# The end of a transformer kernel: last expert's output by halves, look-ahead behind the branch, one residual instruction and one store per tile

## The chip, the cores and the metric

The kernel runs on one core of a Trainium2 chip. The metric is the time of one execution on the device in microseconds (us); lower is better. The engines that matter here are TensorE (PE, matmuls), VectorE (DVE) and ScalarE (ACT) for elementwise work, GpSimd (POOL), and SyncE (SP), which issues transfers. Each runs its own queue of instructions in order; they wait for each other through semaphores.

## The reference

Two layers of a block that mixes differential attention and gated linear attention, for 256 latent tokens beside 256 context tokens, width 1024, fp32. The second layer's feed-forward part is a mixture of 8 experts, two per token. Only its end matters here:

```python
logits = (ht @ router).astype(jnp.float32)
top_v, top_i = lax.top_k(logits, TOP_K)                  # TOP_K = 2 of 8 experts
wts = jax.nn.softmax(top_v, axis=-1)
combine = jnp.sum(one_hot(top_i, 8) * wts[..., None], axis=1)
def expert_step(acc, p):
    e1, e3, e2, cw = p                                   # 1024x2816, 1024x2816, 2816x1024
    return acc + cw[:, None] * swiglu(ht, e1, e3, e2), None
out, _ = lax.scan(expert_step, jnp.zeros_like(ht), (w1, w3, w2, combine.T))
x = x + gt2 * rms_norm(out, g_post_ffn[l])               # out: 256 x 1024, the result is x
```

`rms_norm(y, g)` is y * rsqrt(mean(y*y) + 1e-6) * g, the mean over the 1024 columns of a token. In the kernel gt2 * g is one row, `gate`, copied to all partitions.

## The kernel before, in words

Tokens lie on the 128 partitions, so 256 tokens are two tiles (t = 2 and 3 of `X`, tt = 0 and 1 of `y_moe`). Matmuls run in fp32r with each operand split in a high and a low part: `three` (L1444) does hi*hi, hi*lo, lo*hi, three matmuls of 128x512. ACT makes high parts (`high`, L917: w_hi <- raw), DVE low parts (`low`, L1327: raw minus w_hi).

**Experts.** Weights come in units of 128x2048 (1 MB), 33 per expert, through 5 places for raw data and 4 for split ones. An expert is one pass p over at most 128 of its tokens; three extra passes (8, 9, 10) exist for experts with more. A pass has 11 column chunks g: `up_chunk` (two units into a PSUM bank), ACT's silu, DVE's product, PE's transposes (`turn_chunk`), `down_chunk` (one unit: 12 matmuls that add to the two PSUM banks of the pass, one for each half of 512 output columns). PE starts by gathering the pass's tokens and later scatters the output back.

**Look-ahead.** ACT and DVE split the unit that is 4 ahead of the one just used: `high(ahead(...))` and `low(ahead(...))` in `run`. Behind the last down chunk of a run they so split a unit of the next pass, though nothing may need it.

**Output of a pass** (`output`, L937 and L1341): ACT copies each half out of PSUM as ey_hi, DVE makes ey_lo. PE multiplies both by the transposed selection (`scatter`, L1796), four pieces n = 2*tt + h, and DVE adds each, times the token's weight, to `y_moe` (`added`, L1349). For passes 0 to 7 this happens inside the next pass.

**Runs and the branch.** Passes 0 to 7 are one run; each extra pass is a run of its own inside nested `If(run_valid(eng, k))` (L492): the engine loads a register from `task_i` (`TENSOR_LOAD`), tests it and branches. Every engine has its own such branch. In the `Else` stands the end: the last output, four scatters into four banks, four accumulations.

**The tail.** `mean_square` (L675 Square with sums to `ssq`, L678 Sqrt) on ACT; `residual` (L1227) on DVE: reciprocal, y * rstd * gate, and for tile 3 the addition to X; POOL adds tile 2 (L578); SP stores both tiles in one transfer (L567).

The order of the instructions on each engine is the order of the code; no scheduler changes it.

## Time and profile before

| | us |
|---|---|
| three timed runs | 2032.96, 2034.84, 2035.08 |
| their median | 2034.84 |
| the profiled execution, its own time | 2033.05 |
| its span in the trace | 2030.9 |

| engine | busy us | share of the span |
|---|---|---|
| PE | 1885.3 | 93% |
| DVE | 1242.8 | 61% |
| ACT | 1068.4 | 53% |
| POOL | 43.6 | 2% |

The rows further down come from one profiled execution. All times in them are us from the start of its span unless marked ns. The engines overlap, so shares of busy time don't add up to the span; a serial stretch shows as idle times that end with another engine's instruction.

### The profile page before, as it was taken

How to read it: one execution, taken by the hardware profiler on the slowest of the kernel's cores; microseconds unless marked ns; L12 is line 12 of the kernel's file. 1: busy time of each engine (PE TensorE's matmuls, PEld its weight loads, DVE VectorE, ACT ScalarE, POOL GpSimd, SP SyncE). 2: the span in 40 equal slices, each digit the busy share in tenths (PEclk: the TensorE clock that was granted, in tenths of full speed). 3: DMA queues.
4: the chain of work that ended last, by engine and by line, in shares of the span. 5: the costliest groups of instructions: out<-in, count | busy, mean ns of one | idle time of the engine just before them, and what ended most of it. 6: DMA issues, size and time to landing. Idle time of an engine off the chain costs nothing.

```text
span 2030.9 us, 25112 instructions
## 1 busy us (share of the span) xinstructions
PE 1885.3 (93%) x10056; PEld 1536.4 (76%) x10056; DVE 1242.8 (61%) x1379; ACT 1068.4 (53%) x1368; POOL 43.6 (2%) x38
## 2 busy tenths in 40 slices
PE   6999889979999997998886999999999999999995
PEld 4877567968888786876666888888888888888784
DVE  3232752453223334433645889898989898898886
ACT  4323542352222224424634777777777777676764
POOL 0000000000000000000001020000000000000000
PEclk9999875989999999999967999999999999999997
DMA  8312643212332222223712899998999998999994
GB/s 340 104 58 72 227 156 112 83 63 83 104 104 83 104 84 83 90 82 117 278 52 115 326 351 365 344 364 343 365 343 363 345 362 347 359 344 341 351 334 163
DMA packets 61528, 441.84 MB, mean 218 GB/s; under 512 B 6836, under 2 KB 6964, under 8 KB 8288
## 3 DMA queue, kind: packets, MB, share of 16 engines
q1 hardware_dynamic: 60032, 436.23, 57.3%
q10 hardware_dynamic: 1120, 3.28, 0.4%
q8 instruction: 83, 1.36, 0.3%
q0 software_dynamic: 256, 0.66, 0.1%
q14 instruction: 37, 0.30, 0.0%
HBM read 439.10 MB, written 1.05 MB: 217 GB/s over the span
## 4 chain that ended last, share of the span: by engine, by line
PE 83%; DVE 10%; ACT 4%; DMA 1%; issue 1%; SPq 0%; DVEq 0%; ACTq 0%
PE psum L1447 72%; PE psum L1789 2%; DMA raw<-units 1%; PE psum L1665 1%; DVE act_lo L1089 1%; PE psum L1671 1%; PE psum L1832 1%; PE psum L1464 1%; DVE row_max L1169 1%; PE psum L1805 1%; ACT probs L774 1%; PE psum L1470 1%; DVE states L1200 1%; DVE y_mix L1238 1%; DVE act_hi L1087 1%
## 5 line engine op out<-in xcount | busy, mean ns | idle before, releaser
L1332 DVE TENSOR_TENSOR w_lo<-raw,w_hi 128x2048 fp32r<-128x2048 f32 x136 | 311.0, 2290 | 50.8 <-ACT w_hi L923 50.3
L923 ACT ACTIVATE w_hi<-raw 128x2048 fp32r<-128x2048 f32 x136 | 261.0, 1920 | 107.2 <-PE psum L1447 104.6
L1025 DVE TENSOR_TENSOR w_lo<-raw,w_hi 128x1024 fp32r<-128x1024 f32 x130 | 153.4, 1221 | 233.1 <-ACT w_hi L630 233.1
L1447 PE MATMUL psum<-w_hi,xt_hi 128*128 128x512 f32 x596 | 233.6, 392 | 2.7 <-DVE xt_lo L1337 2.7
L1447 PE MATMUL psum<-w_hi,xt_lo 128*128 128x512 f32 x596 | 232.7, 390 | 0.0
L1447 PE MATMUL psum<-w_lo,xt_hi 128*128 128x512 f32 x596 | 232.6, 390 | 0.0
L1332 DVE TENSOR_TENSOR w_lo<-raw_more,w_hi 128x2048 fp32r<-128x2048 f32 x90 | 206.0, 2290 | 34.9 <-ACT w_hi L923 34.5
L630 ACT ACTIVATE w_hi<-raw 128x1024 fp32r<-128x1024 f32 x130 | 130.2, 1051 | 156.9 <-PE psum L1447 151.5
L923 ACT ACTIVATE w_hi<-raw_more 128x2048 fp32r<-128x2048 f32 x90 | 172.9, 1921 | 74.5 <-PE psum L1447 74.5
L1447 PE MATMUL psum<-act_hi,w_hi 128*128 128x512 f32 (+1 forms) x544 | 208.4, 383 | 2.1 <-DVE act_lo L1089 1.9
L1447 PE MATMUL psum<-act_lo,w_hi 128*128 128x512 f32 (+1 forms) x544 | 207.2, 381 | 0.0
L1447 PE MATMUL psum<-act_hi,w_lo 128*128 128x512 f32 (+1 forms) x544 | 207.1, 381 | 0.0
L1447 PEld LDWEIGHTS psum<-w_hi,xt_hi 128*128 128x128 f32 x596 | 112.3, 188 | 26.2 <-DVE xt_lo L1337 3.1
L1447 PEld LDWEIGHTS psum<-w_hi,xt_lo 128*128 128x128 f32 x596 | 112.3, 188 | 23.5
L1447 PEld LDWEIGHTS psum<-w_lo,xt_hi 128*128 128x128 f32 x596 | 112.3, 188 | 23.0
L1447 PE MATMUL psum<-w_hi,act_hi 128*128 128x256 f32 (+1 forms) x368 | 126.0, 343 | 2.1 <-DVE act_lo L1089 1.7
L1447 PE MATMUL psum<-w_lo,act_hi 128*128 128x256 f32 (+1 forms) x368 | 123.8, 337 | 0.0
L1447 PE MATMUL psum<-w_hi,act_lo 128*128 128x256 f32 (+1 forms) x368 | 123.7, 336 | 0.0
L1447 PE MATMUL psum<-w_hi,eT_hi 128*128 128x512 f32 x296 | 122.2, 413 | 0.0
L1447 PEld LDWEIGHTS psum<-act_hi,w_hi 128*128 128x128 f32 x544 | 102.8, 189 | 23.8 <-DVE act_lo L1089 4.7
L1447 PEld LDWEIGHTS psum<-act_hi,w_lo 128*128 128x128 f32 x544 | 103.0, 189 | 19.3
L1447 PEld LDWEIGHTS psum<-act_lo,w_hi 128*128 128x128 f32 x544 | 102.9, 189 | 19.2
(260 smaller groups left out, 3505.8 us busy)
## 6 DMA issues: line engine op xcount, KB each, us to landing
raw<-units SPq DMA_DIRECT2D x295, 1024.0 KB, 4.9
raw_more<-units SPq DMA_DIRECT2D x120, 1024.0 KB, 5.0
X<-ctx_in ACTq DMA_DIRECT2D x1, 1024.0 KB, 16.4
X<-x_in ACTq DMA_DIRECT2D x1, 1024.0 KB, 23.2
out<-X SPq DMA_DIRECT2D x1, 1024.0 KB, 4.1
const<-const_in ACTq DMA_DIRECT2D x1, 520.0 KB, 9.5
rope<-rope_in POOLq DMA_DIRECT2D x2, 256.0 KB, 5.5
wsm<-wsm_in ACTq DMA_DIRECT2D x1, 288.0 KB, 26.8
```

The lines of the kernel that those rows point to most:

```text
L630: act.activation(w_hi[:, i % RING, part], raw[:, i % RING, part], ACT.Copy).then_inc(hi_ready, 1)
L774: act.activation(probs[:, b, j, 0:keys], bank(("S", l, i, j))[:, 0:keys], ACT.Exp, scale=QK ** -0.5, bias=neg_max[:, b, j:j + 1], accum_ou ...
L923: act.activation(w_place(m)[0], raw_place(m), ACT.Copy).then_inc(esem("w_high"), 1)
L1025: ins = dve.tensor_tensor(w_lo[:, i % RING, part], raw[:, i % RING, part], w_hi[:, i % RING, part].bitcast(F32), ALU.subtract)
L1087: dve.tensor_copy(act_hi[:, k, lo:T], hf[:, k % RING, lo:T]).then_inc(sem(f"act_hi_{stage}{l}"), 1)
L1089: dve.tensor_tensor(act_lo[:, k, lo:T], hf[:, k % RING, lo:T], act_hi[:, k, lo:T].bitcast(F32), ALU.subtract).then_inc(sem(f"act_lo_{stage ...
L1169: ins = dve.tensor_reduce(row_max[:, b, j:j + 1], bank(("S", l, i, j))[:, 0:keys], X_AXIS, ALU.max)
L1200: ins = dve.scalar_tensor_tensor(states[:, dp, after, :], states[:, dp, here, :], decay[:, dp, here:here + 1], ds, ALU.mult, ALU.add)
L1238: dve.scalar_tensor_tensor(y(t), y(t), rstd[:, t:t + 1], gate[:, w, 0 if t < 2 else 1, :], ALU.mult, ALU.mult).then_inc(sem(f"y_{stage}{l} ...
L1332: dve.tensor_tensor(lo, raw_place(m), hi.bitcast(F32), ALU.subtract).then_inc(esem("w_ready"), 1)
L1447: ins = pe.matmul(dst, lhs(a), rhs(b), start=first and n == 0, stop=last and n == 2)
L1789: ins = pe.matmul(psum[:, down_bank(p, n), (k % 4) * P:(k % 4 + 1) * P], src[:, tt, k * P:(k + 1) * P], chosen[:, tt, :], start=i == 0, st ...
```

## The change

In words:

- `down_chunk`, all chunks: half 0's six matmuls first, then half 1's; the last chunk of a pass signals after half 0 (`out_half`). ACT's `output` waits for that for half 0, and for the whole chunk for half 1 only. `scatter` waits for the ey_lo of its own half.
- In the last chunk of each run the look-ahead split is left out; it is made inside the `If`, where a pass follows. The last pass's output stands ahead of the branch on ACT and DVE.
- The squares of the last norm are taken per half, right behind each accumulation; ACT loads the table for the root before them. The gate is multiplied per half on DVE, and normalisation and residual are one instruction per tile, X = y * rstd + X, both on DVE. POOL has no part in it.
- SP stores each tile when it is ready.

```diff
--- before.py
+++ after.py
@@ -181,6 +181,10 @@
 UNIT_LIST = pass_units()
 UNIT_AT = {key: m for m, key in enumerate(UNIT_LIST)}
 RUN_END = tuple((passes[-1] + 1) * EXPERT_UNITS for passes in RUNS)
+
+
+def run_last(r):
+    return (RUNS[r][-1] + 1) * FC - 1
 
 
 def unit_of_expert(key):
...
@@ -562,10 +569,10 @@
 
         extra_loads(0)
 
-        for t in token_tiles(1, "out"):
+        for n, t in enumerate(token_tiles(1, "out")):
             sp.wait_ge(x_added("ffn", 1, t), 1)
-        sp.dma_start(out[0].rearrange("(t p) d -> p t d", p=P), X[:, CTX // P:TILES, :]).then_inc(stored, 16)
-        sp.wait_ge(stored, 16)
+            sp.dma_start(out[0, n * P:(n + 1) * P, :], X[:, t, :]).then_inc(stored, 16)
+        sp.wait_ge(stored, 32)
 
 
     @block.gpsimd
@@ -610,7 +617,6 @@
                 pool.wait_ge(sem("tasks"), 1)
                 for extra in range(EXPERTS, PASSES_OF):
                     select(extra)
-        add(1, "ffn", y_moe_of)
 
 
     @block.scalar
@@ -936,10 +942,13 @@
 
         def output(p):
 
-            wait_used(act, ("down", p * FC + FC - 1))
             if p:
                 act.wait_ge(esem("scattered"), 4 * p)
             for h in range(2):
+                if h == 0:
+                    act.wait_ge(esem("out_half"), p + 1)
+                else:
+                    wait_used(act, ("down", p * FC + FC - 1))
                 act.activation(ey_hi[:, h * 512:(h + 1) * 512], psum[:, down_bank(p, h), :], ACT.Copy).then_inc(
                     esem("ey_hi"), 1)
 
@@ -964,16 +973,17 @@
                 p, c = divmod(up, FC) if up is not None else (None, None)
                 if up is not None:
                     high(ahead(("up", up, 0)))
-                    if c == (2 if p < EXPERTS else 0) and p:
+                    if c == 2 and 0 < p < EXPERTS:
                         output(p - 1)
                     high(ahead(("up", up, 1)))
                     silu(up)
                 if turned is not None:
                     columns_turned(turned)
-                if down is not None:
+                if down is not None and down != run_last(r):
                     high(ahead(("down", down)))
                 if c == GATHER_STEP and p + 1 < PASSES_OF:
                     columns_high(p + 1)
+            output(RUNS[r][-1])
 
         for m in range(W_RING):
             if m < RING:
@@ -985,19 +995,33 @@
         columns_high(0)
         run(0)
 
+        def finish(p):
+
+            act.activation(std[:, 0:1], eps, ACT.Sqrt).then_inc(sem("root_table"), 1)
+            for n in range(4):
+                tt, h = divmod(n, 2)
+                act.wait_ge(esem("added"), 4 * p + n + 1)
+                if n >= 2:
+                    act.wait_ge(sem("final_square"), n - 1)
+                act.activation(y_junk[:, h * 512:(h + 1) * 512], y_moe[:, tt, h * 512:(h + 1) * 512], ACT.Square,
+                               accum_out=y_part[:, 2 + tt, h:h + 1]).then_inc(sem("final_square"), 1)
+
         def extra(k):
             with act.If(run_valid(act, k)):
+                high(RUN_END[k] + W_RING - 1)
                 run(k + 1)
                 if k + 1 < EXTRA:
                     extra(k + 1)
                 else:
-                    output(EXPERTS + k)
+                    finish(EXPERTS + k)
             with act.Else():
-                output(EXPERTS + k - 1)
+                finish(EXPERTS + k - 1)
 
         extra(0)
-        act.wait_ge(sem("summed"), 1)
-        mean_square("post", 1, "ffn", (2, 3), y_moe_of, lambda t: y_junk[:, :], lambda n: None)
+        for n, t in enumerate(token_tiles(1, "out")):
+            act.wait_ge(sem("final_sum"), n + 1)
+            act.activation(y_std[:, t:t + 1], y_ssq[:, t:t + 1], ACT.Sqrt, bias=eps, scale=1.0 / D_MODEL).then_inc(
+                sem("final_std"), 1)
 
 
     @block.vector
@@ -1378,7 +1402,7 @@
                 p, c = divmod(up, FC) if up is not None else (None, None)
                 if up is not None:
                     low(ahead(("up", up, 0)))
-                    if c == (2 if p < EXPERTS else 0) and p:
+                    if c == 2 and 0 < p < EXPERTS:
                         output(p - 1)
                     if p and SCATTER_STEP < c <= SCATTER_STEP + 4:
                         added(p - 1, c - SCATTER_STEP - 1, SCATTER_BANK)
@@ -1386,7 +1410,7 @@
                     product(up)
                 if turned is not None:
                     columns_turned(turned)
-                if down is not None:
+                if down is not None and down != run_last(r):
                     low(ahead(("down", down)))
                 if c == GATHER_STEP and p + 1 < PASSES_OF:
                     columns_low(p + 1)
@@ -1396,6 +1420,7 @@
                     next_task(c - 3)
                 if p == 0 and c == 3 + EXTRA:
                     dve.tensor_copy(task_i[:, :], task[:, :]).then_inc(sem("tasks"), 1)
+            output(RUNS[r][-1])
 
         def ranked():
 
@@ -1417,15 +1442,25 @@
         columns_low(0)
         run(0)
 
+        def gated_half(n):
+
+            tt, part = n // 2, slice((n % 2) * 512, (n % 2 + 1) * 512)
+            dve.wait_ge(sem("final_square"), n + 1)
+            dve.tensor_tensor(y_moe[:, tt, part], y_moe[:, tt, part], gate[:, 1, 1, part], ALU.mult).then_inc(
+                sem("final_gate"), 1)
+
         def finish(p):
-            output(p)
-            for n in range(4):
-                added(p, n, n)
-            dve.wait_ge(esem("added"), 4 * p + 4)
-            dve.sem_inc(sem("summed"), 1)
+            added(p, 0, 0)
+            added(p, 1, 1)
+            added(p, 2, 2)
+            dve.wait_ge(esem("added"), 4 * p + 4 - 1)
+            gated_half(0)
+            added(p, 3, 3)
+            gated_half(1)
 
         def extra(k):
             with dve.If(run_valid(dve, k)):
+                low(RUN_END[k] + W_RING - 1)
                 run(k + 1)
                 if k + 1 < EXTRA:
                     extra(k + 1)
@@ -1434,9 +1469,27 @@
             with dve.Else():
                 finish(EXPERTS + k - 1)
 
+        for h in range(2):
+            wait_copied(dve, ("GB", 1, 1, 1, h))
         extra(0)
-        dve.wait_ge(sem("summed"), 1)
-        residual(1, "ffn", y_moe_of)
+
+        def tile_sum(n, t):
+            dve.wait_ge(sem("final_square"), 2 * n + 2)
+            dve.tensor_reduce(y_ssq[:, t:t + 1], y_part[:, t, 0:2], X_AXIS, ALU.add).then_inc(sem("final_sum"), 1)
+
+        def tile_out(n, t):
+            dve.wait_ge(sem("final_std"), n + 1)
+            link(dve.reciprocal(y_rstd[:, t:t + 1], y_std[:, t:t + 1]))
+            dve.wait_ge(sem("final_gate"), 2 * n + 2)
+            dve.scalar_tensor_tensor(X[:, t, :], y_moe[:, n, :], y_rstd[:, t:t + 1], X[:, t, :], ALU.mult, ALU.add).then_inc(
+                x_added("ffn", 1, t), 1)
+
+        tile_sum(0, 2)
+        gated_half(2)
+        tile_out(0, 2)
+        tile_sum(1, 3)
+        gated_half(3)
+        tile_out(1, 3)
 
 
     @block.tensor
@@ -1796,7 +1849,7 @@
         def scatter(p, n, bank_of):
 
             tt, h = divmod(n, 2)
-            pe.wait_ge(esem("ey_lo"), 2 * p + 2)
+            pe.wait_ge(esem("ey_lo"), 2 * p + h + 1)
             pe.wait_ge(esem("selT_copy"), min(p + 2, PASSES_OF))
             before = 4 * p + (n if bank_of == SCATTER_BANK else 0)
             if before:
@@ -1837,11 +1890,13 @@
             p, c = divmod(g, FC)
             pe.wait_ge(esem("eT_lo"), g + 1)
             both = unit_ready(("down", g))
-            for j in range(2):
-                for h in range(2):
+            for h in range(2):
+                for j in range(2):
                     ins = three(psum[:, down_bank(p, h), :], lambda a: (eT_hi, eT_lo)[a][:, g % 2, j * P:(j + 1) * P],
                                 lambda b: both[b][:, j * D_MODEL + h * 512:j * D_MODEL + (h + 1) * 512],
                                 c == 0 and j == 0, c == FC - 1 and j == 1)
+                if c == FC - 1 and h == 0:
+                    ins.then_inc(esem("out_half"), 1)
             ins.then_inc(esem("w_used"), 1)
 
         def run(r):
```

Two places where the queues change. ACT at the end of pass 8, up to its second branch and what follows the jump; before (w_hi<-raw are splits, ey_hi the output's halves, `COMPARE_AND_BRANCH` the branch; the pass's last three splits, then the branch, then what the `Else` holds further down):

```order
L958 ACTIVATE eT_hi<-psum 128x256 [waits e_w_used,e_turned]
L923 ACTIVATE w_hi_more<-raw_more_121 128x2048 [waits more_arrived4,e_w_used]
L923 ACTIVATE w_hi<-raw 128x2048 [waits more_arrived0,e_w_used]
L495 TENSOR_LOAD task_i [waits tasks]
L495 ISA x2
L989 COMPARE_AND_BRANCH
...
L943 ACTIVATE ey_hi<-psum 128x512 [waits e_scattered,e_w_used]
L943 ACTIVATE ey_hi<-psum 128x512
L995 UNCONDITIONAL_BRANCH
```

The same place on ACT now:

```order
L967 ACTIVATE eT_hi<-psum 128x256 [waits e_w_used,e_turned]
L929 ACTIVATE w_hi_more<-raw_more_121 128x2048 [waits more_arrived4,e_w_used]
L952 ACTIVATE ey_hi<-psum 128x512 [waits e_out_half,e_scattered]
L952 ACTIVATE ey_hi<-psum 128x512 [waits e_w_used]
L502 TENSOR_LOAD task_i [waits tasks]
L502 ISA x2
L1010 COMPARE_AND_BRANCH
...
L1000 ACT_TABLE_LOAD
L1000 ACTIVATE std<-const 128x1
L1006 ACTIVATE y_junk,y_part<-y_moe 128x512 [waits e_added] x2
L1006 ACTIVATE y_junk,y_part<-y_moe 128x512 [waits final_square,e_added] x2
L1017 UNCONDITIONAL_BRANCH
```

One split left the queue, the two copies moved ahead of the branch, and the `Else` holds the table load and the squares. DVE's queue moves in the same way up to its branch. DVE from the `Else` to its end, before (y_moe<-psum are the accumulations, L1434 the end of the `Else`):

```order
L1346 TENSOR_TENSOR ey_lo<-psum,ey_hi 128x512 [waits e_ey_hi] x2
L1358 SCALAR_TENSOR_TENSOR y_moe<-psum,route,y_moe 128x512 [waits e_added,tasks,e_scattered] x4
L1434 UNCONDITIONAL_BRANCH [waits e_added]
...
L1237 RECIPROCAL rstd<-std 128x1 [waits emptied3,post_ffn1,emptied2,summed]
L1238 SCALAR_TENSOR_TENSOR y_moe<-y_moe,rstd,gate 128x1024 [waits dve_step]
L1237 RECIPROCAL rstd<-std 128x1 [waits post_ffn1]
L1238 SCALAR_TENSOR_TENSOR y_moe<-y_moe,rstd,gate 128x1024 [waits dve_step]
L1242 TENSOR_TENSOR X<-X,y_moe 128x1024 [waits y_ffn1]
```

And now (y_moe<-y_moe,gate are the gate products, y_ssq the sums of two halves):

```order
L1382 SCALAR_TENSOR_TENSOR y_moe<-psum,route,y_moe 128x512 [waits e_added,tasks,e_scattered] x3
L1449 TENSOR_TENSOR y_moe<-y_moe,gate 128x512 [waits final_square,e_added]
L1382 SCALAR_TENSOR_TENSOR y_moe<-psum,route,y_moe 128x512 [waits e_added,tasks,e_scattered]
L1449 TENSOR_TENSOR y_moe<-y_moe,gate 128x512 [waits final_square]
L1469 UNCONDITIONAL_BRANCH
...
L1478 TENSOR_REDUCE y_ssq<-y_part 128x1 [waits final_square]
L1449 TENSOR_TENSOR y_moe<-y_moe,gate 128x512 [waits final_square]
L1482 RECIPROCAL y_rstd<-y_std 128x1 [waits final_std]
L1484 SCALAR_TENSOR_TENSOR X<-y_moe,y_rstd,X 128x1024 [waits final_gate,dve_step]
...
```

The last four rows stand twice, once per tile. Two gate products lie between the accumulations and the branch's end, and a tile's last instruction writes X itself.

## Rows read from the trace of the kernel before

**Rows 1.** The page, busy us, share of the span and instructions of each engine:

```profile
PE 1885.3 (93%) x10056; PEld 1536.4 (76%) x10056; DVE 1242.8 (61%) x1379; ACT 1068.4 (53%) x1368; POOL 43.6 (2%) x38
```

**Rows 2.** Busy time by stretches: us, each engine (instructions), granted clock, DMA share, GB/s:

```profile
1600.00:1700.00 100.00, 100.00 (x470) 82.99 (x469) 88.80 (x64) 72.83 (x63) 1.89 (x2) 1.00 0.93 354
```

**Rows 3.** One line's instructions, ACT's branch: duration ns min/median/max, first and last start:

```profile
L989 ACTq COMPARE_BRANCH  x2: 49/50/50, 1904.3 to 2006.4; - x2
```

**Rows 4.** Timeline of the tail: start, us, engine, line, operation, [idle before, its releaser]:

```profile
2004.79 2.29 DVE L1332 TENSOR_TENSOR w_lo_more<-raw_more,w_hi_more 128x2048 fp32r<-128x2048 f32 x1 [4.07 <-ACT w_hi_more L923]
...
2005.38 0.39 PE L1447 MATMUL psum<-w_hi,eT_lo 128*128 128x512 f32 x1
2005.81 1.91 ACT L923 ACTIVATE w_hi<-raw 128x2048 fp32r<-128x2048 f32 x1 [1.05 <-PE psum L1447]
2007.75 2.29 DVE L1332 TENSOR_TENSOR w_lo<-raw,w_hi 128x2048 fp32r<-128x2048 f32 x1 [0.67 <-ACT w_hi L923]
2009.00 1.09 ACT L943 ACTIVATE ey_hi<-psum 128x512 fp32r<-128x512 f32 x2 [1.29 <-issue]
2009.96 1.28 DVE L1346 TENSOR_TENSOR ey_lo<-psum,ey_hi 128x512 fp32r<-128x512 f32 x2
...
2011.29 0.80 PE L1805 MATMUL psum<-ey_hi,selT 128*128 128x512 f32 x1 [5.53 <-DVE ey_lo L1346]
...
2012.55 2.46 DVE L1358 SCALAR_TENSOR_TENSOR y_moe<-psum,route,y_moe 128x512 f32<-128x512 f32 x3 [1.31 <-PE psum L1805]
...
2016.39 0.75 DVE L1358 SCALAR_TENSOR_TENSOR y_moe<-psum,route,y_moe 128x512 f32<-128x512 f32 x1 [1.38 <-PE psum L1805]
...
2018.40 1.28 ACT L678 ACT_TABLE_LOAD   x1
...
2020.12 0.16 DVE L1237 RECIPROCAL rstd<-std 128x1 f32<-128x1 f32 x1 [2.98 <-ACT std L678]
2020.32 1.28 DVE L1238 SCALAR_TENSOR_TENSOR y_moe<-y_moe,rstd,gate 128x1024 f32<-128x1024 f32 x1
...
2021.69 2.34 POOL L578 TENSOR_TENSOR X<-X,y_moe 128x1024 f32<-128x1024 f32 x1 [345.86 <-DVE y_moe L1238]
2021.71 3.39 DVE L1238 SCALAR_TENSOR_TENSOR y_moe<-y_moe,rstd,gate 128x1024 f32<-128x1024 f32 x1
2025.14 1.22 DVE L1242 TENSOR_TENSOR X<-X,y_moe 128x1024 f32<-128x1024 f32 x1
2026.46 0.41 SPq L567 DMA_DIRECT2D out<-X  x1
```

**Rows 5.** The page's DMA issues: tiles, engine, count, KB, median us to landing:

```profile
out<-X SPq DMA_DIRECT2D x1, 1024.0 KB, 4.1
```

**Rows 6.** Busy time by stretches, the tail:

```profile
1998.00:2006.00 8.00, 7.53 (x26) 5.73 (x26) 3.93 (x4) 2.56 (x4) 0.00 (x0) 0.79 0.15 60
2006.00:2012.00 6.00, 0.71 (x2) 0.61 (x3) 4.57 (x4) 2.80 (x3) 0.00 (x0) 0.82 0.02 4
...
2026.50:2031.00 4.50, 0.00 (x0) 0.00 (x0) 0.00 (x0) 0.00 (x0) 0.00 (x0) 0.50 0.58 233
```

**Rows 7.** Chain of waits behind DVE's test; PE's jump at the branch's end:

```profile
2008.46 1.50 issue
...
L1876 PEldq COMPARE_BRANCH  x1: 193/193/193, 2015.2 to 2015.2; - x1
```

**Rows 8.** Timeline at the boundary before pass 8, and in the last down chunk:

```profile
1903.53 1.92 ACT L923 ACTIVATE w_hi_more<-raw 128x2048 fp32r<-128x2048 f32 x1 [0.80 <-PE psum L1447]
...
1911.49 0.39 PE L1447 MATMUL psum<-w_hi_more,xt_hi 128*128 128x512 f32 x1
...
1914.48 0.48 PE L1447 MATMUL psum<-w_hi,xt_hi 128*128 128x512 f32 x1
...
2004.69 0.39 PE L1447 MATMUL psum<-w_hi,eT_lo 128*128 128x512 f32 x1
...
2004.92 0.40 PE L1447 MATMUL psum<-w_hi,eT_hi 128*128 128x512 f32 x1
```

More of the change, by code:

```diff
@@ L398, in build @@
     ssq, std, rstd = stat("ssq", 4), stat("std", 4), stat("rstd", 4)
+    y_part = at("y_part", stat_at[0], [P, TILES, OUT_UNITS])
+    stat_at[0] += 16
+    y_ssq, y_std, y_rstd = stat("y_ssq", 4), stat("y_std", 4), stat("y_rstd", 4)
     modc = at("modc", stat_at[0], [P, DEPTH, N_MOD, KT, 2])
```

## The prediction

> **What bounds the kernel now.** I read the page first, then the busy time by stretches, then the timeline and the chain of waits of the last 30 us. By the page TensorE (PE) is busy 93% of the span [rows 1]; in a stretch inside the expert stage it is busy 100.00 of 100 us at full granted clock, with VectorE (DVE) at 88.80 and the DMA engines at 0.93 [rows 2]. A gain there needs fewer matmul cycles, and the change takes none away. The last 25 us are another program: little overlaps, one engine at a time hands work on, and behind the eight scatter matmuls PE has nothing to do. So the change is worth what it takes out of the serial tail, less what it does to the work before it.
>
> An expert that more than 128 tokens chose gets an extra pass. The test for this runs twice here, at 1904.3 and 2006.4 on ACT [rows 3]: the first lets one extra pass run, the second jumps out. So nine passes run, 99 column chunks, and the tail follows pass 8, behind a jump.
>
> The tail of before, from the timeline [rows 4]. PE's last expert matmul starts at 2005.38 and is done at 2005.77. ACT then splits a unit that no pass will use (2005.81, 1.91 us), jumps, and copies ey_hi at 2009.00. DVE makes the low part of the same useless unit (2007.75, 2.29 us) and starts ey_lo at 2009.96. PE adds back from 2011.29; DVE's fourth accumulation ends at 2016.39 + 0.76 = 2017.15. Then squares, table load (1.28), root, gate and residual until 2025.14 + 1.22 = 2026.36, and the store at 2026.46, 4.1 us to landing [rows 5].
>
> **The change, part by part.** Times are of the profiled execution: span 2030.9, own time 2033.05, so 2.15 us lie around the span. The median of the three timed runs is 2034.84; with the profiled one the four average 2033.98. I take the gain off that average.
>
> *Look-ahead removed from the end.* ACT's split of 1.91 us and DVE's of 2.29 us go. What is late next is the split of the unit before, which stays: DVE at 2004.79, 2.29 us, done 2007.08. As now, ey_lo can start 0.08 before that end, at 2007.00 (now 2009.96). ACT's copies are ready earlier: the first by about 2005.4, the second at about 2006.4, two taking 1.09. Gain 2.96. It also shows that the *copy of half 0 ahead of PE's last six matmuls* is worth nothing by itself: DVE is busy until 2007.08 either way. Without that split it would be worth up to 1.0.
>
> *Scatter waits per half.* Two ey_lo take 1.28 us; PE starts 1.33 after their start [rows 4]. Now it starts after the first, 0.64 + 0.04 = 0.68. Gain 0.65; PE's first scatter starts at 2007.68.
>
> *Scatter and accumulation.* From PE's start to the end of the fourth accumulation it is 2017.15 - 2011.29 = 5.86 us. The instructions and the fourth scatter's wait for the third accumulation stay. The new gate product on half 0 stands ahead of the fourth accumulation in DVE's queue; but DVE idles there anyway, 1.38 us [rows 4], and the product takes about 0.69 (below). That product waits for its square, behind ACT's jump (2009.00), a table load (1.28), a root and the square, for which I set 1.1 by the 1.09 of two copies of that size: 2011.4, when the third accumulation ends too (1.38 before the fourth starts). Cost 0, with 0.7 us of cover. Fourth accumulation over at 2013.54.
>
> *From there to the store.* Now 2026.46 - 2017.15 = 9.31; in it DVE's second product of 3.39 us, against 1.28 for the same form, while POOL adds (2021.69, 2.34) [rows 4]. POOL has nothing in the new tail. DVE's new queue is: gate product, sum, gate product, reciprocal, residual, sum, gate product, reciprocal, residual. A 128x512 product of two SBUF operands is in no row; 2048 columns take 2.29 and 1024 take 1.22, so 1.07 per 1024 and 0.69 for 512. The bounds are 0.61 (half of 1.22) and 1.22 (no shorter). A sum of two columns I take as the reciprocal, 0.17. From the reciprocal's start to the product's 2020.32 - 2020.12 = 0.20, a product of three operands 1.28. So 0.69 + 0.17 + 0.69 + 0.20 + 1.28 + 0.17 + 0.69 + 0.20 + 1.28 = 5.37, and 0.10 to SP's issue: 5.47. Gain 3.84; by the bounds 4.08 or 2.25. ACT's last square ends about 0.8 after the fourth accumulation and the first root some 0.4 later, and DVE comes to the reciprocal at 1.55. The table load is out of the chain, under the scatters. The second store issues at 2019.01.
>
> *Stores.* In the 4.5 us behind 2026.5 the DMA engines are busy for a share of 0.58, 2.61 us, at a mean of 233 GB/s, the store's 1.05 MB [rows 6]; 4.1 - 2.61 = 1.49 us is not data. Tile 2's store goes at about 2016.6 and its data is out before the last one's begins. The last half megabyte: 1.49 + 1.31 = 2.80. Gain 1.30; the low bound is 0 (half takes the whole 4.1 too). The Trainium skill (DMA: Bandwidth & Descriptors, Rules for kernel authors) speaks against splitting: coalesce, and 1 MiB or more per DMA for bandwidth. With the fixed cost of about 2.0 us that the same page gives, the last store would take 3.3, an estimate by that page, and the sum would be 0.5 smaller; this case's row leaves 1.49.
>
> *The jump.* DVE must be past its jump for the first accumulation, at 2007.68 + 1.26 = 2008.94 (now 2012.55 behind 2011.29). Its test starts when the instruction before it is dispatched: now the test is over at 2008.46, 0.71 after the split started, and ey_lo starts 1.50 later [rows 7]. With the second ey_lo dispatched at about 2007.04, DVE is ready at 2009.25 at the latest by this row, 0.3 late; it could be on time, since DVE was still busy at 2009.96. ACT needed 2009.00 - 2006.45 = 2.55 [rows 3, 4]. By that DVE is ready at 2010.30, and three accumulations of 0.75 in a row end at 2012.55 in place of 2011.40: 1.1 late. I take 0 and keep 1.1.
>
> *Before the tail.* The order within a down chunk changes (half 0's six matmuls, then half 1's), with the same 12. Now the bank changes every third matmul, for one at 2004.92, and the pitch is 0.23 across the change and inside a bank [rows 4, 8]: cost 0. At the boundary before pass 8 the look-ahead moves behind the test, and output(7) ahead of it. ACT's split of that unit was at 1903.53; now two copies (1.09) and the test come first, so about 1904.7 to 1906.6, and DVE's 2.29 after it. PE uses the unit at 1911.49 [rows 8], 2.6 us later. Cost 0.
>
> *Clock.* In 2006 to 2012 the mean granted clock is 0.82 [rows 6]: full for 3.84 us, then half, from about 2009.8, 4 us after PE's last expert matmul. The new scatters run from 2007.68, so three of them might still get 2.4 GHz. At full clock the first matmul after a break takes 0.48, not 0.80 [rows 4, 8]. It would save up to 0.7, if DVE is ready; I take 0 and keep 0.7 for the lower end.
>
> Sum: 2.96 + 0.65 + 3.84 + 1.30 = 8.75. Span 2022.1, profiled 2024.3; against the average of four, 2033.98 - 8.75 = **2025.2**.
>
> **Rivals.**
> 1. *A jump in the open.* The tail has two new places where an engine's jump is not covered: DVE's first accumulation, and the jump at the end of the branch, between the last gate product in it and the first sum (on ACT: the last square and the first root). For: ACT's 2.55 us. Against: PE's jump at that same end took 0.19 [rows 7]. Price 1.1 (DVE late once) to 2.55 (the end jump): gain 6.2 to 7.65, so 2026.3 to 2027.8. The Trainium skill (Runtime: NRT & Kernel Launch, Instruction fetch mechanics) has this as a rule: a taken branch whose target is outside the fetched window stalls until that page is fetched. By it the long jump out costs and the short end jump need not; ACT's 2.55 and PE's 0.19 agree with it.
> 2. *The second store lands no sooner*, 4.1 again: gain 7.45, 2026.5. For: only one store is in the trace, so the split of its 4.1 is inferred. Against: the data's rate.
> 3. *The boundary before pass 8 stalls PE.* If the test took ACT's 2.55 there, ACT's split would start at about 1907.1 and end at 1909.0, and DVE's three splits behind it, back to back, at 1915.9. The activation product comes after them, where PE had its next matmul at 1914.48 [rows 8]: some 2 us late, and after such a wait about 3.4 us ran at half clock (0.79 over 1998 to 2006 [rows 6]), 1.7 more. Gain 5.1, 2028.9. Against: that test doesn't jump, and PE never waited behind it.
> 4. *Slower: the order in the down chunks.* Place: 99 chunks. Behind the transposes a matmul takes 0.48, not 0.39 [rows 8]. If the new order cost one such 0.09 per chunk, 99 x 0.09 = 8.9 eats the gain (2034.1); two make 2043. It decides from 0.09 per chunk. Against: the bank change of now costs nothing, so having fewer should not cost either.
> 5. *It doesn't do what it says*: half 0's early copy does nothing, as computed. That is inside the forecast.
>
> **Numbers.** Forecast 66%, its own range 2024.0 to 2026.4 (0.7 of clock, 1.1 of jump, run differences of 1). Rival 1 20%, rival 2 5%, rival 3 4%, rival 4 4% (half of it slower, half no change), 1% other. 0.2% is 4.1 us, about what a measurement tells from nothing, so faster means under 2030.8: 0.94, same 0.03, slower 0.03. Range 2023.2 to 2028.0: the lower end takes the clock and a lucky run, the upper one rivals 1 and 2.
>
> **What would show it.** Right: ey_lo starts directly behind DVE's split at about 2007.0; PE's first scatter 0.7 later; the table load on ACT before the first square; no POOL instruction after the experts; residuals of 1.28; the second store issued 5.5 after the fourth accumulation and landed in 2.8. The clock at the scatters decides the 0.7, the idle time before DVE's first accumulation the 1.1. Wrong: a gap of over 1 us on DVE or ACT between the last gate product in the branch and the first sum; 4.1 at the last store; PE idle between 1903 and 1915; or longer expert chunks, which would end the argument that only the tail moves.

## The result, and the profile after

Median 2025.53 us of five runs, against 2034.84 before (five runs, 2032.96 to 2036.69). One of the five, of 2264.2, was disturbed and is left out of the comparison; the other four lie from 2021.67 to 2026.79, with a median of 2023.78. Their ratio to before is 0.9947, 95% interval 0.9931 to 0.9962: 0.5% faster, clear of noise. The forecast was 2025.2, its range 2023.2 to 2028.0. The profiled execution took 2022.02, its span is 2019.8 us.

Up to the last chunk's silu nothing moved. The silu of the 99 chunks, one line's instructions (duration ns min/median/max, first and last start):

```profile
L960 ACT ACTIVATE e_sil<-psum x99: 358/361/384, 1126.2 to 1995.0; 128x256 f32<-128x256 f32 x99
```

Before, it ran from 1126.1 to 1995.0. What is left is the tail, by its timeline (columns as in [rows 4]), engine by engine. `<-issue` marks idle time whose end nothing in the profile explains; behind a branch it holds the test and the jump. PE:

```profile
2003.72 0.39 PE L1500 MATMUL psum<-w_hi,eT_lo 128*128 128x512 f32 x1
2006.33 0.60 PE L1858 MATMUL psum<-ey_hi,selT 128*128 128x512 f32 x1 [2.21 <-DVE ey_lo L1370]
...
2010.00 0.77 PE L1858 MATMUL psum<-ey_hi,selT 128*128 128x512 f32 x1 [0.94 <-DVE y_moe L1382]
```

ACT:

```profile
2001.43 1.92 ACT L929 ACTIVATE w_hi_more<-raw_more 128x2048 fp32r<-128x2048 f32 x1 [2.39 <-PE psum L1500]
2003.25 0.57 ACT L952 ACTIVATE ey_hi<-psum 128x512 fp32r<-128x512 f32 x1
2004.15 0.60 ACT L952 ACTIVATE ey_hi<-psum 128x512 fp32r<-128x512 f32 x1 [0.32 <-PE psum L1500]
2007.29 1.28 ACT L1000 ACT_TABLE_LOAD   x1 [2.54 <-issue]
...
2008.69 0.61 ACT L1006 ACTIVATE y_junk<-y_moe 128x512 f32<-128x512 f32 x1
...
2012.68 0.29 ACT L1023 ACTIVATE y_std<-y_ssq,const 128x1 f32<-128x1 f32 x1
```

DVE, to the last residual; three rows of tile 3 that repeat the forms of tile 2 are left out:

```profile
2003.38 2.29 DVE L1356 TENSOR_TENSOR w_lo_more<-raw_more,w_hi_more 128x2048 fp32r<-128x2048 f32 x1 [2.69 <-ACT w_hi_more L929]
2005.59 1.28 DVE L1370 TENSOR_TENSOR ey_lo<-psum,ey_hi 128x512 fp32r<-128x512 f32 x2
2007.40 2.46 DVE L1382 SCALAR_TENSOR_TENSOR y_moe<-psum,route,y_moe 128x512 f32<-128x512 f32 x3 [0.53 <-PE psum L1858]
2009.89 0.69 DVE L1449 TENSOR_TENSOR y_moe<-y_moe,gate 128x512 f32<-128x512 f32 x1
2011.23 0.75 DVE L1382 SCALAR_TENSOR_TENSOR y_moe<-psum,route,y_moe 128x512 f32<-128x512 f32 x1 [0.65 <-PE psum L1858]
2011.90 0.68 DVE L1449 TENSOR_TENSOR y_moe<-y_moe,gate 128x512 f32<-128x512 f32 x1
2012.50 0.15 DVE L1478 TENSOR_REDUCE y_ssq<-y_part 128x1 f32<-128x2 f32 x1
2012.57 0.68 DVE L1449 TENSOR_TENSOR y_moe<-y_moe,gate 128x512 f32<-128x512 f32 x1
2013.17 0.15 DVE L1482 RECIPROCAL y_rstd<-y_std 128x1 f32<-128x1 f32 x1
2013.36 1.28 DVE L1484 SCALAR_TENSOR_TENSOR X<-y_moe,y_rstd,X 128x1024 f32<-128x1024 f32 x1
...
2015.41 1.28 DVE L1484 SCALAR_TENSOR_TENSOR X<-y_moe,y_rstd,X 128x1024 f32<-128x1024 f32 x1
```

The stores by the list of DMA issues (KB each, median us to landing):

```profile
out<-X SPq DMA_DIRECT2D x2, 512.0 KB, 2.7
```

Nothing stands any more between the split that stays and ey_lo; the table load lies beside the scatters; from the fourth accumulation to the last residual DVE has no idle time. Below, "M" is the start of PE's last expert matmul, and the tail is the span less M. It was 2030.9 - 2005.38 = 25.52 and is 2019.8 - 2003.72 = 16.08: 9.44 of the span's 11.1. The other 1.66 is M itself, and it goes with TensorE's granted clock. Of before, busy time by stretches (columns as in [rows 2]):

```profile
1996.00:1998.00 2.00, 0.11 (x1) 0.00 (x0) 2.00 (x3) 1.85 (x1) 0.00 (x0) 1.00 0.97 369
...
2000.00:2002.00 2.00, 2.00 (x6) 1.57 (x5) 0.72 (x2) 0.00 (x0) 0.00 (x0) 0.50 0.00 0
...
2010.00:2012.00 2.00, 0.71 (x2) 0.61 (x3) 1.24 (x3) 0.09 (x1) 0.00 (x0) 0.50 0.00 0
```

And of after:

```profile
1996.00:1998.00 2.00, 0.09 (x1) 0.00 (x0) 2.00 (x3) 1.88 (x1) 0.00 (x0) 1.00 0.98 389
...
2000.00:2002.00 2.00, 2.00 (x11) 1.63 (x10) 0.69 (x2) 0.57 (x1) 0.00 (x0) 1.00 0.00 0
...
2006.50:2007.00 0.50, 0.50 (x2) 0.20 (x3) 0.37 (x1) 0.00 (x0) 0.00 (x0) 0.58 0.04 16
2007.00:2008.00 1.00, 1.00 (x3) 0.82 (x3) 0.60 (x1) 0.71 (x1) 0.00 (x0) 0.50 0.04 8
```

PE waits about 2 us for the last chunks' product in both. In before the clock then stood at half (1.2 GHz) while PE worked the last down chunks; in after those ran at full (2.4 GHz), and the clock halved at the scatters, at about 2006.6.

### The profile page after: what moved, and what is told of

The parts are those of the page before. It is cut to its first block, busy times and chain, and to the rows that moved or that the text cites. A ratio compares the mean times of both kernels' runs of the same rounds, so it can differ in the third digit from the quotient of the medians.

```text
span 2019.8 us, 25121 instructions
## 1 busy us (share of the span) xinstructions
PE 1881.6 (93%) x10056; PEld 1534.7 (76%) x10056; DVE 1239.9 (61%) x1383; ACT 1066.2 (53%) x1372; POOL 41.2 (2%) x37
## 4 chain that ended last, share of the span: by engine, by line
PE 83%; DVE 10%; ACT 4%; DMA 2%; issue 1%; DVEq 0%; ACTq 0%
PE psum L1500 72%; PE psum L1842 2%; DMA raw<-units 1%; PE psum L1718 1%; DVE act_lo L1113 1%; PE psum L1724 1%; PE psum L1885 1%; PE psum L1517 1%; DVE row_max L1193 1%; PE psum L1858 1%; ACT probs L780 1%; PE psum L1523 1%; DVE states L1224 1%; DVE y_mix L1262 1%; DVE act_hi L1111 1%
## 5 line engine op out<-in xcount | busy, mean ns | idle before, releaser
L1500 PEld LDWEIGHTS psum<-w_hi,xt_hi 128*128 128x128 f32 x596 | 112.3, 188 | 26.1 <-DVE xt_lo L1361 3.1
```

The source lines that it names most:

```text
L1500: ins = pe.matmul(dst, lhs(a), rhs(b), start=first and n == 0, stop=last and n == 2)
```

## The experiments

Spans aren't compared: the last silu starts anywhere between 1994.6 and 2001.1, with the experts' 868.6 to 868.9 us nearly always the same, so that difference arises before the experts. (Only 4 has 870.3: its granted clock was 0.56 and 0.59 in 1902 to 1906, at the boundary before pass 8, where after has 1.00.) Each profile is read from its last silu on, in us: to M, from M to the start of ey_lo, then to PE's first scatter, to the end of the fourth accumulation, to the end of the last residual, to the end of the span (SP's issue and the landing in it), and in the last two columns the tail from M and the sum.

| kernel | to M | ey_lo | scatter | 4th sum | residual | end | tail | from silu |
|---|---|---|---|---|---|---|---|---|
| before | 10.37 | 4.58 | 1.33 | 5.85 | 9.22 | 4.54 | 25.52 | 35.9 |
| after | 8.74 | 1.87 | 0.74 | 5.65 | 4.71 | 3.11 | 16.08 | 24.8 |
| after, 2nd | 10.33 | 1.64 | 0.74 | 4.76 | 4.71 | 3.10 | 14.96 | 25.3 |
| after, 3rd | 8.72 | 1.87 | 0.73 | 5.63 | 4.72 | 3.09 | 16.04 | 24.8 |
| 1 | 8.73 | 1.86 | 1.34 | 5.35 | 9.23 | 4.56 | 22.34 | 31.1 |
| 2 | 10.35 | 4.58 | 1.34 | 5.84 | 8.37 | 4.57 | 24.70 | 35.1 |
| 3 | 8.72 | 1.87 | 0.74 | 5.64 | 4.71 | 3.06 | 16.02 | 24.7 |
| 4 | 10.30 | 1.87 | 0.74 | 5.37 | 4.71 | 4.51 | 17.20 | 27.5 |
| 5 | 8.75 | 1.86 | 0.74 | 5.71 | 5.93 | 3.12 | 17.36 | 26.1 |
| 6 | 8.73 | 1.86 | 0.74 | 4.32 | 5.44 | 3.09 | 15.45 | 24.2 |
| 7 | 8.73 | -0.24 | 1.98 | 5.59 | 4.71 | 3.11 | 15.15 | 23.9 |
| 8 | 8.74 | -0.24 | 1.50 | 4.45 | 4.72 | 3.09 | 13.52 | 22.3 |
| 9 | 10.68 | -0.25 | 0.75 | 4.14 | 5.43 | 3.11 | 13.18 | 23.9 |
| 10 | 8.74 | -0.24 | 1.98 | 3.48 | 5.43 | 3.09 | 13.74 | 22.5 |

Two values of "to M" return, 8.7 and 10.3 to 10.4: the second is half clock before M, by the granted clock in before, 2 and 4 and in the second profile of after (below); 9 is long for another reason. The changed kernel shows both, so neither value needs an edit. Whether the change makes the long one rarer is not shown: both profiles with the old end (before, 2) have it, and 2 of the 11 with the look-ahead moved, 9 not counted.

**1. Only the look-ahead and the output moved (from before).** ACT's part of the edit; DVE has the same.

```diff
-                if down is not None:
+                if down is not None and down != run_last(r):
                     high(ahead(("down", down)))
...
+            output(RUNS[r][-1])
...
             with act.If(run_valid(act, k)):
+                high(RUN_END[k] + W_RING - 1)
                 run(k + 1)
...
-            with act.Else():
-                output(EXPERTS + k - 1)
```

> The kernel before with one part of the change: the look-ahead split behind the last down chunk of a run goes behind the branch, and ACT's and DVE's output goes ahead of it. Nothing by halves, tail as before. My theory (DVE's split of the unit before is late next): ey_lo starts 0.08 us before the end of DVE's last split, 2.96 us closer to that split's start than now; PE's first scatter 1.33 us after the start of ey_lo, the same rest of the tail; 3.0 us less. Rival (DVE's or ACT's jump comes into the open): DVE's first accumulation waits for its jump, the stretch from PE's first scatter to the end of the first accumulation grows by up to 1.4 us (now 2.02), gain 1.6.

Timed: 2030.81, ratio 0.9981 (0.9969 to 0.9992), a small gain. The tail is 3.18 shorter. Its timeline:

```profile
2007.41 2.29 DVE L1334 TENSOR_TENSOR w_lo_more<-raw_more,w_hi_more 128x2048 fp32r<-128x2048 f32 x1 [2.67 <-ACT w_hi_more L927]
...
2008.18 1.08 ACT L947 ACTIVATE ey_hi<-psum 128x512 fp32r<-128x512 f32 x2 [0.80 <-PE psum L1450]
2009.62 1.28 DVE L1348 TENSOR_TENSOR ey_lo<-psum,ey_hi 128x512 fp32r<-128x512 f32 x2
```

ey_lo starts 2.21 behind the split's start, where it was 5.17 in [rows 4]: 2.96, the predicted size, of which 2.72 shows from M on. The tail's other 0.50 came from the fourth scatter, at full clock here. The first accumulation follows PE by 1.26 as before, so here no jump was in the open.

**2. Only POOL's addition moved to DVE (from before).**

```diff
-        add(1, "ffn", y_moe_of)
...
-                if t % 2:
+                if t % 2 or (l == 1 and stage == "ffn"):
```

> The kernel before with POOL's last addition (tile 2) made by DVE. My theory (POOL's addition stretches DVE's product beside it): DVE's second product takes 1.28 us in place of 3.39, and the addition of 1.22 comes in; from the end of the fourth accumulation to the store's issue 9.31 - 2.11 + 1.22 = 8.4 us. Rival (the 3.39 has another cause, such as waiting for ACT): the product stays at 3.39 and the stretch grows to 10.5.

One run: 2034.41. From DVE's timeline:

```profile
2023.85 1.22 DVE L1241 TENSOR_TENSOR X<-X,y_moe 128x1024 f32<-128x1024 f32 x1
2024.99 0.16 DVE L1236 RECIPROCAL rstd<-std 128x1 f32<-128x1 f32 x1
2025.19 1.28 DVE L1237 SCALAR_TENSOR_TENSOR y_moe<-y_moe,rstd,gate 128x1024 f32<-128x1024 f32 x1
```

The second product takes 1.28 where it took 3.39 beside POOL; 1.22 of addition came in its place, and the tail is 0.82 shorter. So the long product was POOL's doing, and most of the term's gain has other sources: the table load beside the scatters, priced in experiment 5, and one instruction per tile in place of two and a gate product beside the scatters, which no run prices by themselves.

**3. The order of the down chunks and the early copy undone (from after).**

```diff
-            for h in range(2):
-                for j in range(2):
+            for j in range(2):
+                for h in range(2):
...
-                if c == FC - 1 and h == 0:
-                    ins.then_inc(esem("out_half"), 1)
...
                 if h == 0:
-                    act.wait_ge(esem("out_half"), p + 1)
-                else:
                     wait_used(act, ("down", p * FC + FC - 1))
```

> The changed kernel with half 0's early copy undone: the down chunks' matmuls in the old order, and ACT's two copies both wait for the whole chunk. Scatters still wait per half. My theory: the time from DVE's last split to the first ey_lo does not move (ey_lo directly behind the split), 0.0 us, and the 99 chunks take the same time. Rival 1 (the early copy matters): ey_lo starts later than the end of DVE's split, up to 0.6 us. Rival 2 (the order in the chunks costs or saves): the time from 1200 to 1900 us, per chunk, moves by 0.05 us or more, 5 us over 99.

Timed: 2023.97, ratio to before 0.9945 (0.9928 to 0.9961). One line's instructions, as above:

```profile
L958 ACT ACTIVATE e_sil<-psum x99: 359/362/384, 1125.9 to 1994.7; 128x256 f32<-128x256 f32 x99
```

868.8 for the chunks either way, ey_lo 1.87 after M either way: both edits are worth nothing.

**4. One store for both tiles (from after).**

```diff
             sp.wait_ge(x_added("ffn", 1, t), 1)
-            sp.dma_start(out[0, n * P:(n + 1) * P, :], X[:, t, :]).then_inc(stored, 16)
-        sp.wait_ge(stored, 32)
+        sp.dma_start(out[0].rearrange("(t p) d -> p t d", p=P), X[:, CTX // P:TILES, :]).then_inc(stored, 16)
+        sp.wait_ge(stored, 16)
```

> The changed kernel with one store of both tiles at the end. My theory: landing 4.1 us behind the issue in place of 2.7, so 1.4 us more at the end and nothing else. Rival (the stores share a fixed cost, and tile 2's store slows the last one): less than 0.5 us.

One run: 2030.78; its last silu starts 6.1 later than after's, so this time says nothing of the store. The stretch behind the residual is 4.51 against 3.11, and the list of issues has:

```profile
out<-X SPq DMA_DIRECT2D x1, 1024.0 KB, 4.0
```

**5. No early table load (from after).**

```diff
         def finish(p):
-            act.activation(std[:, 0:1], eps, ACT.Sqrt).then_inc(sem("root_table"), 1)
```

> The changed kernel without the early root on ACT that loads its table: the load then stands ahead of the first real root. My theory (the load was covered by the scatters): ACT's first square starts when the first accumulation ends, the load of 1.28 us comes behind the fourth square, the first root ends 1.3 us later than now and DVE's first reciprocal waits for about 1.2 us; the end is 1.1 to 1.3 us later. Rival (ACT's squares were late because of the table, and bound the tail): the gate products come earlier and the end moves by less than 0.5.

One run: 2024.40. From ACT's timeline, behind the last square:

```profile
2013.92 1.28 ACT L1022 ACT_TABLE_LOAD   x1
2015.22 0.29 ACT L1022 ACTIVATE y_std<-y_ssq,const 128x1 f32<-128x1 f32 x1
```

Fourth accumulation to last residual 5.93, not 4.71: 1.22 of the load's 1.28.

**6. The fourth scatter without its wait (from after).** It has a bank of its own, so the wait for the third accumulation protects nothing here.

```diff
-            before = 4 * p + (n if bank_of == SCATTER_BANK else 0)
+            before = 4 * p + (n if bank_of == SCATTER_BANK and not last else 0)
...
-                scatter(p, n, n)
+                scatter(p, n, n, True)
...
             added(p, 2, 2)
-            dve.wait_ge(esem("added"), 4 * p + 4 - 1)
-            gated_half(0)
             added(p, 3, 3)
+            dve.wait_ge(esem("added"), 4 * p + 4)
+            gated_half(0)
             gated_half(1)
```

> The changed kernel, the fourth scatter of the tail not waiting for the third accumulation (its bank is free), and both first gate products behind the fourth accumulation. My theory: PE's eight scatter matmuls run in a row, the fourth accumulation directly behind the third, 1.3 us earlier; the gate product that was hidden comes back with 0.6; the end is 0.6 to 0.7 us earlier. Rival (ACT's squares bound the tail): the end stays within 0.2.

One run: 2020.93. The wait held 1.33 (5.65 to 4.32), of which 0.73 comes back because the gate product that filled DVE's gap now stands behind it. Tail 0.63 shorter.

**7. The unit before also left to the branch (from after).** In the extra runs the last two look-ahead units are split inside the `If`.

```diff
 def run_last(r):
-    return (RUNS[r][-1] + 1) * FC - 1
+    last = (RUNS[r][-1] + 1) * FC - 1
+    return (last,) if r == 0 else (last - 1, last)
...
-                if down is not None and down != run_last(r):
+                if down is not None and down not in run_last(r):
...
-                high(RUN_END[k] + W_RING - 1)
+                for m in left_out(k):
+                    high(m)
```

> The changed kernel; in the extra passes the last two look-ahead splits go behind the branch, not just the last. DVE's split at 2003.38 goes. My theory (PE's data, then the jumps, are late next): ey_lo of half 0 starts once ACT has copied it, some 1.5 us earlier, half 1's at about 4.75 us (counted from 2000) where it was 6.24; PE's jump is over at about 5.2, so the first scatter starts about 1 us earlier; DVE's jump leaves it ready at 7.0 to 7.4 as now, so the first accumulation gains at most 0.4 and the end at most 0.5. Rival (no jump binds): the end is 1.0 to 1.5 us earlier.

One run: 2023.03. ey_lo comes 2.1 earlier, but the tail is only 0.93 shorter. PE's branch (one line's instructions), then its timeline's first scatter, which DVE no longer holds; then ACT and DVE further down it:

```profile
L1932 PEldq COMPARE_BRANCH  x2: 86/1926/3766, 1903.1 to 2003.5; - x2
```

```profile
2007.39 0.47 PE L1865 MATMUL psum<-ey_hi,selT 128*128 128x512 f32 x1 [1.35 <-DVE ey_lo L1376]
...
2009.42 1.28 ACT L1005 ACT_TABLE_LOAD   x1 [2.75 <-issue]
...
2011.63 0.69 DVE L1455 TENSOR_TENSOR y_moe<-y_moe,gate 128x512 f32<-128x512 f32 x1 [1.43 <-ACT y_junk L1011]
```

PE's compare without a jump took 0.086, with one 3.77: 2003.5 + 3.77 = 2007.27, and the scatter starts at 2007.39, though half 0's ey_lo was done at 2006.10. Then ACT's jump delays table load and squares, and DVE waits 1.43 for a square. Two engines' jumps bind, one after the other. The third doesn't: the expectation put the limit on DVE's jump, but DVE's first accumulation waited for PE, 0.73. Beside the second profile of after (below 9), whose scatters also ran at full clock, the tail is no shorter (15.15 against 14.96): what 7 gains from the silu on, 0.9, goes with the clock, at full through the scatters, which follow PE's last matmul after 1.35 idle and not 2.21.

**8. As 7, with the branch ahead of the output on ACT and DVE.**

```diff
                     columns_high(p + 1)
-            output(RUNS[r][-1])
...
             with act.If(run_valid(act, k)):
+                output(RUNS[k][-1])
...
         def finish(p):
-
+            output(p)
```

> As the kernel before it in this list (two units behind the branch), and on ACT and DVE the test and the jump come ahead of the last output, so that they lie under PE's last down chunk. My theory (jumps of 2.5 us on ACT and up to 1.9 us on DVE bind the start of the accumulations): ACT's table load directly behind its second copy, the first accumulation directly behind PE's first scatter at about 6 us (from 2000) in place of 7.4, the end 1.3 to 2.0 us earlier than in the changed kernel. Rival (only PE's and DVE's work binds): no difference to the kernel with two units alone.

One run: 2025.15, M 2009.48. Its timeline:

```profile
2009.91 0.60 ACT L957 ACTIVATE ey_hi<-psum 128x512 fp32r<-128x512 f32 x1 [0.70 <-PE psum L1508]
2010.52 1.28 ACT L1004 ACT_TABLE_LOAD   x1
...
2010.74 0.47 PE L1866 MATMUL psum<-ey_hi,selT 128*128 128x512 f32 x1 [0.87 <-DVE ey_lo L1376]
```

ACT's load follows its copy at once: the jump now lies in ACT's idle time before the copies. Only PE's is left. The tail is 2.56 shorter than after's, 1.44 than that of its second profile.

**9. As 8, with 6, and PE's last down chunk behind its branch.**

```diff
-                if down is not None:
+                if down is not None and down != run_last(r)[-1]:
                     down_chunk(down)
...
         def finish(p):
+            down_chunk(p * FC + FC - 1)
             for n in range(4):
-                scatter(p, n, n)
+                scatter(p, n, n, True)
...
             with pe.If(run_valid(pe, k)):
+                down_chunk(run_last(k)[-1])
```

> All that helped in the tail, put together: two look-ahead units behind the branch in the extra passes, the test and jump ahead of the last output on ACT and DVE, on PE ahead of the last down chunk, the fourth scatter without its wait, gate products behind the four accumulations. My theory (PE's jump was the last thing in the open, ending 1.05 us after the start of the last expert matmul): PE's first scatter starts 0.5 us after that start, the second at 1.8 when ey_lo of half 1 is there, the fourth accumulation ends at about 4.7 (8.3 in the changed kernel), and from there 5.4 to the last residual. From the start of the last expert matmul to the end of the span 13.2 us, against 16.1 in the changed kernel and 13.5 with the early branch alone. Rival (half 1's copy and ey_lo keep PE from starting early, so PE's jump was not what held it): first scatter at 1.3 again, 13.5 or more in all.

And with it, on the same chip, the changed kernel again:

> The changed kernel once more, to be timed beside the one above and beside the kernel before. My theory: the tail, from the start of the last expert matmul to the end of the span, is 16.1 us again within 0.3 in the profiled execution, 9.4 less than before; what differs between executions by up to 5 us lies ahead of it, in how long the granted clock is at half. Rival (the tail itself differs between executions): it moves by more than 0.5.

Timed in the same rounds: this one 2025.00, ratio 0.9952 (0.9939 to 0.9966); the changed kernel 2023.30, 0.9942 (0.9928 to 0.9955). No gain. From PE's timeline:

```profile
2003.16 0.39 PE L1508 MATMUL psum<-w_hi_more,eT_lo 128*128 128x512 f32 x1
2005.23 0.47 PE L1508 MATMUL psum<-w_hi,eT_hi 128*128 128x512 f32 x1 [1.68 <-issue]
...
2007.82 0.39 PE L1508 MATMUL psum<-w_hi,eT_lo 128*128 128x512 f32 x1
2008.32 0.50 PE L1866 MATMUL psum<-ey_hi,selT 128*128 128x512 f32 x1
```

The scatter now stands 0.50 behind M, but PE's jump has moved in front of the last chunk, 1.68 in the open. Against 8 the way to M is 1.94 longer and the scatter comes 0.76 sooner behind M: a net loss.

The second profile of the changed kernel went against what was written for it: its tail differs from the first by 1.12, not by under 0.3, with 0.89 between first scatter and fourth accumulation. Busy time by stretches in it:

```profile
2002.00:2004.00 2.00, 2.00 (x6) 1.51 (x6) 0.00 (x0) 0.38 (x1) 0.00 (x0) 0.52 0.04 8
...
2008.00:2010.00 2.00, 1.48 (x6) 0.97 (x6) 1.77 (x4) 0.29 (x1) 0.00 (x0) 1.00 0.02 8
```

The clock was at half before M and at full in the scatters. Counted from the silu M came 1.59 later, and the tail was 1.12 shorter. So what one profile of this kernel loses on one side of M it wins back in part on the other.

**10. As 8, with 6 (PE's last chunk where it was).** The edits are those of 8 and 6.

> Experiment 8 with the fourth scatter's wait left out (as in experiment 6), PE's last down chunk left where it was. Theory (only PE's jump binds at the first scatter, and nothing is put ahead of the last expert matmul): first scatter 1.2 to 1.4 us after the start of the last expert matmul; at full clock four accumulations in a row, the first 0.74 after the scatter, so the fourth ends 0.74 + 3 x 0.67 + 0.75 = 3.50 after it; residual 5.43 later; 3.1 to the end. Tail 13.2 to 13.4 us at full clock at the scatters, against 14.96 of the changed kernel at full clock there, and no idle time of PE ahead of the last down chunk. The time should then be about 1.6 us, 0.08%, under the changed kernel's in the same rounds, which five rounds can hardly tell. Rival (as in experiment 9, what goes from the tail comes back before it): a gap of over 1 us on PE before the last expert matmul, or a time at or above the changed kernel's.

With it in the same rounds:

> The changed kernel a third time, as the measure for the kernel beside it. By the theory that the granted clock decides the tail: about 16.0 us from the last expert matmul's start if the clock halves at the scatters, about 15.0 if it halved before them. A tail outside 14.8 to 16.3, or one of about 15 with half clock at the scatters, would speak against it.

Timed: 2020.13 (six runs, 2019.88 to 2025.29), ratio to before 0.9937 (0.9922 to 0.9952); the changed kernel 2024.76 (2023.06 to 2026.45), 0.9952 (0.9939 to 0.9965). The median is 4.6 under, the mean 3.3; the intervals of the two ratios overlap. Its timeline:

```profile
2004.16 0.39 PE L1508 MATMUL psum<-w_hi,eT_lo 128*128 128x512 f32 x1
...
2005.90 0.47 PE L1866 MATMUL psum<-ey_hi,selT 128*128 128x512 f32 x1 [1.35 <-DVE ey_lo L1376]
...
2006.65 2.73 DVE L1388 SCALAR_TENSOR_TENSOR y_moe<-psum,route,y_moe 128x512 f32<-128x512 f32 x4 [0.74 <-PE psum L1866]
```

Four accumulations in a row end 3.48 after the scatter, as expected, and PE isn't idle before M. The scatter stands 1.74 behind M, not 1.2 to 1.4: PE's jumping compare took 3.82 here and 3.34 in 8. That is why the tail is 13.74 and not 13.3. From the silu on it is 2.3 shorter than after's, but 0.2 longer than 8's: between the first scatter and the last residual the edit of 6 gained 0.26 on 8 (8.91 against 9.17), and PE's longer compare took 0.48. That the edit of 6 adds to 8 in the whole is therefore not shown. The third profile of after (16.04, clock falling at its scatters) is on the forecast's first figure.

## Why the prediction was right

| term | predicted | measured |
|---|---|---|
| look-ahead removed | 2.96 | 2.71 from M; 2.96 from DVE's split |
| scatter waits per half | 0.65 | 0.59 |
| scatter and accumulation | 0 | 0.20 |
| fourth accumulation to issue | 3.84 | 4.64 |
| stores | 1.30 | 1.30 |
| sum | 8.75 | 9.44 |

- **What is late next** was read rightly: the split that stays. ey_lo starts 2.21 behind it, 0.08 before its end. Against M it is 0.25 less, because the split started 0.34 before M in after and 0.59 before; experiment 1 shows both figures without the other edits. That half 0's early copy is worth nothing followed from the same row, and experiment 3 shows it.
- **Scatter and accumulation**: the gate product took DVE's gap as written (idle 0.65 in place of 1.38), cost nothing, and experiment 6 shows what the gap hides. The 0.20 is the first scatter pair, partly still at full clock.
- **The mis-sized term** is the stretch from the fourth accumulation to the issue: predicted 5.47, measured 4.68 (4.71 to the residual's end, issue 0.03 before it). Every duration was right: 0.68 for the gate product (0.69 set), 0.15 for the sum (0.17), 1.28 for the residual. The step "0.69 + 0.17 + 0.69 + 0.20 + ..." is what failed: it adds whole durations. In the trace an instruction that doesn't need its neighbour's result starts before that one ends: gate product to sum 0.60 (0.69 set), sum to gate product 0.07 (0.17), gate product to reciprocal 0.60 (0.69), residual to the next sum 1.20 (1.28). Over the nine instructions that makes 0.66, and 0.13 at the issue. The rows of before had shown it (ey_lo starting 0.08 before the split's end, used for the first term) and it wasn't applied here.
- **Stores**: the second lands in 2.7 (2.80 predicted), experiment 4 gives 4.0 for the single one. The low bound of 0 fell, and with it rival 2. The Trainium skill (DMA: Bandwidth & Descriptors, Anatomy of one DMA — SWDGE (gpsimd) path) gives a fixed cost of about 2.0 us, for transfers that GpSimd issues; it would have put the last landing at 3.3, an estimate. This store is issued by SP and landed in 2.7, so the measurement decides for the 1.49 that this case's row leaves. The same page of the Trainium skill (Rules for kernel authors) asks for 1 MiB or more per DMA for bandwidth; for the last transfer of this program two of half that size paid 1.3.
- **The jump** (rival 1) stayed covered: DVE's first accumulation waited for PE, 0.53. The end jump took no time: the compare-free jump at the branch's end and the first sum stand inside the chain (2011.90, 2012.50). Only one thing was late, without a cost: ACT's squares, since its jump took 2.54 again. The first came at 2008.69, 0.5 behind the first accumulation, but DVE doesn't ask for it before 2009.89. Experiment 7 shows the rival's mechanism once the cover is gone, on PE and ACT, not on DVE, where the forecast had priced it. The Trainium skill's rule (Runtime: NRT & Kernel Launch, Instruction fetch mechanics), that a taken branch out of the fetched window stalls, fits: 0.086 against 3.77 on PE. That this target lay outside the window is in no row.
- **Before the tail**: rivals 3 and 4 fell, by the silu's first and last start (868.8 against 868.9), by experiment 3, and by ACT's idle time of 0.29 behind the test that doesn't jump.
- **Clock**: kept as 0.7 for the lower end, taken as 0 in the sum. Measured between two profiles of the same kernel: 0.89 in the scatters, and 1.6 before M, which the forecast had not seen as a chance of its own. Of the 11.1 between the two profiled spans 1.66 is that. The single profiles don't show whether it is chance: over the three sets of timed runs that hold both kernels the means lie 10.9, 11.8 and 9.9 apart, nearer on average to 11.1 than to the tail's 9.44, though the interval of each set covers both.

So the tail's gain was 0.7 too small in the sum, by the 0.8 of the mis-sized term. The mechanism held in every term; how near the number came is partly luck. The gain in time was about 10.8, some 2 more than the 8.75, but the base of 2033.98, an average of four, was low too: before averages 2034.8 in those three sets. And the median of 2025.53 flatters it: the changed kernel's means in the three sets are 2024.0 (of the four runs), 2023.2 and 2024.8, 0.4 to 2.0 under the forecast and no lower than the lower end of its range.

What stays open: where before the experts the executions part by up to 6 us (the first silu starts between 1125.9 and 1132.0); what decides on which side of M the half clock falls, and whether the change shifts the odds; and how much of the 4.6 between 10 and the changed kernel is the edit's: 2.3 shows from the silu on, the rest may be that difference before the experts.

## What to carry to other kernels

In a serial tail, ask of every instruction that goes what else ends at the same time: here 4.2 us of useless splits were worth 2.7 to 3.0, since another unit's split stood behind them. Sum a chain of short instructions by the starts of neighbouring rows, not by durations; over the nine here that made 0.66 us. Compare variants by a stretch that begins at a common instruction ahead of the change, and look at the granted clock on both sides before a difference under 2 us is believed. Put an engine's far branch where the engine would wait anyway: ahead of ACT's and DVE's output it helped (8), ahead of PE's queued chunk it cost more than it gave (9).

## What the runs showed of the hardware

- A branch that jumps far costs per engine, and not little: ACT sat 2.14 to 2.75 us, against 0.29 behind its test that doesn't jump; PE's compare took 3.3 to 3.9 us where the same compare without a jump took 0.086. DVE's jump never came into the open. The time runs from the moment the engine comes to the branch, so on ACT it was free where ACT would have waited anyway (8), and on PE 1.68 of it stood in the open where work was queued behind it (9).
- The jump at the end of a branch, to instructions close by, cost nothing that shows between two DVE instructions 0.60 apart.
- A store of 1 MB landed in 4.0 to 4.1 us, one of 0.5 MB in 2.7, when the half before it was out.
- A three-operand product of 128x1024 in SBUF took 3.39 us on DVE beside a POOL addition and 1.28 without.
- The granted clock halved at different places in executions of the same kernel: between 2000 and 2004, before the last expert matmul, or from 2006.6, at the scatters. Where the idle time between that matmul and the scatters was 1.35 us or less (7 to 10), all eight scatter matmuls took 0.39 to 0.50. So they did once after 1.99 idle, in the second profile of the changed kernel; after 2.21 they took 0.60 to 0.77 in its first.
